# A two-layer block on one core: the scan's decays, factors of k and first inverse computed elsewhere

## The reference, cut to what matters

```python
def rwkv7_scan(r, w, k, v, kk, a):        # 16 heads of 64, 512 steps
    def step(state, inp):
        r_t, w_t, k_t, v_t, kk_t, a_t = inp
        sa = jnp.einsum('bhvk,bhk->bhv', state, -kk_t)
        state = (state * w_t[:, :, None, :] + sa[..., None] * (kk_t * a_t)[:, :, None, :]
                 + v_t[..., None] * k_t[:, :, None, :])
        return state, jnp.einsum('bhvk,bhk->bhv', state, r_t)
```

## Time and profile before

| what | us |
| --- | --- |
| runs, median of 3 | 2411.03 |
| lowest and highest run | 2410.76, 2415.05 |
| the profiled execution, its time | 2415.91 |
| its span in the profile | 2414.1 |
| PE busy | 2265.8 |
| DVE busy | 1255.7 |
| ACT busy | 934.1 |
| POOL busy | 830.2 |

### The profile page before, as it was taken

How to read it: one execution, slowest core, us unless ns; L and a number is a source line. 1 busy time by engine, 2 the same in 40 slices (tenths; PEclk the granted TensorE clock), 3 DMA queues, 4 the chain that set the end, 5 groups by cost and what they waited for, 6 DMA issues and landing times.

```text
span 2414.1 us, 46358 instructions
## 1 busy us (share of the span) xinstructions
PE 2265.8 (94%) x19576; PEld 1705.2 (71%) x19576; DVE 1255.7 (52%) x2027; ACT 934.1 (39%) x1665; POOL 830.2 (34%) x456
## 2 busy tenths in 40 slices
PE   8999999999978998888888899999998999999998
PEld 6886778888866647777777747877887766763476
DVE  5028254022164576777777515695313899736123
ACT  4238434233244433444444423464323222344133
POOL 2310334344313115444444203344441433430246
PEclk9999999999979998999999999999997999999999
DMA  4312222232302210000000122244221333222232
GB/s 143 118 51 78 70 70 88 94 99 86 105 25 78 96 42 3 10 10 10 10 10 10 38 70 70 96 183 133 94 87 63 129 113 114 87 87 79 70 90 84
DMA packets 49883, 180.71 MB, mean 75 GB/s; under 512 B 5600, under 2 KB 5856, under 8 KB 49440
## 3 DMA queue, kind: packets, MB, share of 16 engines
q1 hardware_dynamic: 46064, 166.89, 21.4%
q10 hardware_dynamic: 3632, 11.08, 1.2%
HBM read 167.39 MB, written 10.55 MB: 74 GB/s over the span
## 4 chain that ended last, share of the span: by engine, by line
PE 72%; issue 12%; DVE 7%; ACT 4%; POOL 3%; DMA 1%; POOLq 0%; ACTq 0%; SPq 0%; DVEq 0%
PE ps L596 15%; PE ps L597 15%; PE ps L598 15%; PE ps L599 6%; POOL ring_lo L2224 3%; PE ps L858 2%; PE ps L897 2%; PE ps L644 2%; PE ps L1093 1%; PE ps L888 1%; PE ps L925 1%; PE ps L715 1%; PE ps L730 1%; PE ps L705 1%; PE ps L1036 1%
## 5 line engine op out<-in xcount | busy, mean ns | idle before, releaser
L2224 POOL TENSOR_TENSOR ring_lo<-ring,ring_hi 128x1024 fp32r<-128x1024 f32 x232 | 566.0, 2448 | 1018.3 <-ACT ring_hi L1150 1018.2
L598 PE MATMUL ps<-u_lo,ring_hi 128*128 128x512 f32 x968 | 384.7, 397 | 0.0
L1150 ACT ACTIVATE ring_hi<-ring 128x1024 fp32r<-128x1024 f32 x232 | 243.3, 1053 | 113.2 <-DMA ring<-in_wall 109.9
L599 PE MATMUL ps<-arena,ring 128*128 128x512 f32 x608 | 266.1, 594 | 6.4 <-ACT arena L1595 3.3
L599 PEld LDWEIGHTS ps<-arena,ring 128*128 128x128 f32 x608 | 114.4, 190 | 154.3 <-issue 138.6
L596 PE MATMUL ps<-mlp_u_hi,ring_hi 128*128 128x512 f32 x512 | 204.9, 400 | 12.3 <-DVE u_lo L1712 8.2
L598 PEld LDWEIGHTS ps<-u_lo,ring_hi 128*128 128x128 f32 x968 | 183.8, 190 | 43.5
L596 PE MATMUL ps<-mid_hi,ring_hi 128*128 128x512 f32 x512 | 203.3, 397 | 2.6 <-POOL ring_lo L2224 2.6
L597 PE MATMUL ps<-mlp_u_hi,ring_lo 128*128 128x512 f32 x512 | 203.6, 398 | 0.0
L598 PE MATMUL ps<-mid_lo,ring_hi 128*128 128x512 f32 x512 | 202.5, 396 | 0.0
L597 PE MATMUL ps<-mid_hi,ring_lo 128*128 128x512 f32 x512 | 202.5, 395 | 0.0
(11 more groups left out here) (425 smaller groups left out, 4331.0 us busy)
## 6 DMA issues: line engine op xcount, KB each, us to landing
ring<-in_wall SPq DMA_DIRECT2D x273, 512.0 KB, 3.6
s_tables<-arena ACTq DMA_DIRECT2D x16, 512.0 KB, 2.8
arena<-s_tables SPq DMA_DIRECT2D x16, 512.0 KB, 3.6
arena<-bias_lines SPq DMA_DIRECT2D x16, 448.0 KB, 4.3
arena<-in_lora SPq DMA_DIRECT2D x8, 384.0 KB, 3.1
h<-in_x SPq DMA_DIRECT2D x1, 2048.0 KB, 8.1
out<-arena ACTq DMA_DIRECT2D x8, 256.0 KB, 2.9
consts<-in_consts SPq DMA_DIRECT2D x1, 1216.0 KB, 14.4
```

The costliest lines, as they stand in the source:

```text
L598: return nc.tensor.matmul(y, w_hi, low, start=False, stop=x == k - 1)
L599: return nc.tensor.matmul(y, ring[:, at:at + P], rhs(x), start=x == 0, stop=x == k - 1)
L1150: nc.scalar.activation(ring_hi[:, slot], ring[:, slot], ACT.Copy).then_inc(sem("weights_high"), 1)
L2224: G.tensor_tensor(ring_lo[:, slot], ring[:, slot], ring_hi[:, slot].bitcast(F32), ALU.subtract).then_inc(sem("weights_split"), 1)
```

## The change

The exponential of the decay up to the position before is no longer computed: within a chunk it is the neighbour's `ro`, and 1 at the chunk's first position. DVE reads `ro` shifted by one position when it makes `al`, and writes the chunk's first position (the last for the flipped direction) by itself. So the subtraction L1973 and the exponential L1421 go. The two exponentials left per direction are moved on ACT from levels 3 and 4 to behind the u copies of steps 0 to 3. The factor in `kd` is made by ACT (Identity with scale and bias) in level 5 behind the copy of v, in place of DVE in level 4; ACT waits there for `with_bonus` of the previous pair, since that pair's bonus lies in the same buffer. DVE's remaining feature steps move from after steps 3 to 5 to after steps 4 to 6. The predicated copy reads L from PSUM, still behind ACT's copy, and direction 0 is transposed before direction 1 is placed.

```diff
-            def decays(n, F, d):
-                act.wait_ge(sem("decay_summed"), n(2, d + 1))
-                nc.scalar.activation(F[d]["ka"], F[d]["ro"], ACT.Exp, scale=DECAY).then_inc(sem("decays_ready"), 1)
-                nc.scalar.activation(F[d]["al"], F[d]["al"], ACT.Exp, scale=-DECAY).then_inc(sem("decays_ready"), 1)
-                act.wait_ge(sem("decays_ready"), n(6, 3 * d + 1))
-                nc.scalar.activation(F[d]["ro"], F[d]["ro"], ACT.Exp, scale=-DECAY).then_inc(sem("decays_ready"), 1)
+            def decay(n, F, d, step):
+                if step == 0:
+                    act.wait_ge(sem("decay_scanned"), n(2, d + 1))
+                    nc.scalar.activation(F[d]["ka"], F[d]["ro"], ACT.Exp, scale=DECAY).then_inc(sem("decays_ready"), 1)
+                else:
+                    act.wait_ge(sem("decays_ready"), n(4, 2 * d + 1))
+                    nc.scalar.activation(F[d]["ro"], F[d]["ro"], ACT.Exp, scale=-DECAY).then_inc(sem("decays_ready"), 1)
+
+            def kd_factors(n, F):
+                for d in range(2):
+                    act.wait_ge(sem("z_taken"), n(6, 3 + d))
+                    nc.scalar.activation(F[d]["kd"], F[d]["be"], ACT.Identity, scale=pair_col("k_a", n),
+                                         bias=der[:, bass.ds(n(1, OMKA), 1)]).then_inc(sem("kd_factor"), 1)
...
             take_value(6)
-            for d in range(2):
-                decays(first, feats[0], d)
+            for k in range(4):
+                decay(first, feats[0], k // 2, k % 2)
+            kd_factors(first, feats[0])
             features(first, feats[0], 2)
...
                         ins.then_inc(sem("v_turned"), 1)
-                    if nxt and l in (3, 4):
-                        decays(nxt, G, l - 3)
+                        if prev:
+                            act.wait_ge(sem("with_bonus"), prev(2, 2))
+                        if nxt:
+                            kd_factors(nxt, G)
...
                                              ).then_inc(sem("u_taken_too"), 1)
+                    if nxt and j < 4:
+                        decay(nxt, G, j // 2, j % 2)
...
                     elif step == 1:
-                        dve.wait_ge(sem("decay_scanned"), n(2, d + 1))
-                        TT(r["al"], r["ro"], r["al"], ALU.subtract).then_inc(sem("decay_summed"), 1)
+                        dve.wait_ge(sem("decays_ready"), n(4, 2 * (d + 1)))
+                        V_.tensor_copy(ends_at[d], ends(r["ro"], d)).then_inc(sem("p_end_ready"), 1)
                     elif step == 2:
-                        dve.wait_ge(sem("z_taken"), n(6, 3 + d))
-                        TS(r["kd"], r["be"], pair_col("k_a", n), der[:, bass.ds(n(1, OMKA), 1)], ALU.mult, ALU.add
-                           ).then_inc(sem("kd_factor"), 1)
-                    elif step == 3:
-                        dve.wait_ge(sem("decays_ready"), n(6, 3 * (d + 1)))
-                        V_.tensor_copy(ends_at[d], ends(r["ro"], d)).then_inc(sem("p_end_ready"), 1)
-                    elif step == 4:
-                        STT(out=r["al"], in0=r["al"], scalar=-1.0, in1=pair_tile(kk, n), op0=ALU.mult, op1=ALU.mult
-                            ).then_inc(sem("al_ready"), 1)
+                        to, at, first = [(slice(1, CH), slice(0, CH - 1), 0), (slice(0, CH - 1), slice(1, CH), CH - 1)][d]
+                        al, by = chunks(r["al"]), chunks(pair_tile(kk, n))
+                        STT(out=al[:, :, to], in0=chunks(r["ro"])[:, :, at], scalar=-1.0, in1=by[:, :, to],
+                            op0=ALU.mult, op1=ALU.mult)
+                        TS(al[:, :, first], by[:, :, first], -1.0, None, ALU.mult).then_inc(sem("al_ready"), 1)
                     else:
                         dve.wait_ge(sem("p_end_ready"), n(2, d + 1))
+                        dve.wait_ge(sem("al_ready"), n(2, d + 1))
...
                     V_.copy_predicated(chunks(R[d]["TT"]), mask("level", d * LEVELS).bitcast(mybir.dt.int32),
-                                       chunks(R[d]["L"])).then_inc(sem("tt_started"), 1)
-                for d in range(2):
+                                       chunks(bank(4 * d + 1))).then_inc(sem("tt_started"), 1)
                     dve.wait_ge(sem("tt_started"), n(2, d + 1))
                     V_.transpose(R[d]["T"], R[d]["TT"]).then_inc(sem("t_started"), 1)
...
-                    if nxt and l in (1, 2):
-                        features(nxt, G, p_end[1 - parity], l - 1)
+                    if nxt and l == 1:
+                        features(nxt, G, p_end[1 - parity], 0)
...
-                        if nxt:
-                            features(nxt, G, p_end[1 - parity], 2)
...
-                    if nxt and 3 <= j < 6:
-                        features(nxt, G, p_end[1 - parity], j)
+                    if nxt and 4 <= j < 7:
+                        features(nxt, G, p_end[1 - parity], j - 3)
...
-                        pool.wait_ge(sem("decays_ready"), n(6, 3 * (d + 1)))
+                        pool.wait_ge(sem("decays_ready"), n(4, 2 * (d + 1)))
```

More of the change, by code:

```diff
@@ L2086, in pair @@
                         out_bonus(n, F, j // 2)
-                    if nxt and 3 <= j < 6:
-                        features(nxt, G, p_end[1 - parity], j)
+                    if nxt and 4 <= j < 7:
+                        features(nxt, G, p_end[1 - parity], j - 3)
             first, last = (lambda per, c=0: c), (lambda per, c=0: (DT - 1) * per + c)
-            for step in range(6):
+            for step in range(4):
                 features(first, feats[0], p_end[0], step)
```

## The result

The changed kernel takes 2418.97 us, the median of 12 runs, beside 2410.9 for the kernel before in the same session. The ratio is 1.0026, with a 95% interval of 1.0015 to 1.0037: by this ratio it is slower by 6.3 us (0.0026 of 2410.9), over the 0.2% that can be told, where 3.9 us less were forecast. The forecast range ended at 2416.5. The profiled execution took 2419.43 us, near its median.

The account below looks back on a forecast made before the run. PE, busy 94% of the span, was taken as the bound. Terms -10.5 -0.7 -4.0 +5.5 +2.5 +3.3 sum to -3.9 us, giving 2407.1 us against the median 2411.03; range 2400.0 to 2416.5.

Parts of the forecast that it names:

- Part 1: Start of each inverse: copy from PSUM and earlier transpose let PE start sooner; -1.5 us a pair, -10.5 in seven.
- rival E: Start of each inverse: predicated copy as slow from PSUM, gain there only -4.2; total 2413.4 us, chance 0.12.
- Parts 2 and 3: Inverse levels: subtraction between levels 2 and 3 gone, -0.7 us; exponentials out of levels 3 and 4, -4.0 us.
- part 3: Level 5: PE's wait for ACT's copy behind three exponentials goes; -4.0 us, bounds -5.1 and -2.0.
- Part 4: Ahead of step 0's w copy: factors of k on ACT delay PE; +0.8 us a pair, +5.5 in seven.
- Part 5: State steps: POOL's later features slow step 3's decays, +0.4; together +0.35 us a pair, +2.5 in seven.
- Part 6: First pair, outside the loop: later factor delays POOL's features and first L858; +3.3 us, bounds +2.3 and +5.0.
- Rival C: State steps 1 and 3: POOL blocks DVE's decays, 18.9 us in place of 2.5; total 2423.5 us, chance 0.08.
- rival D: ACT's Identity needs a table load of its own in seven pairs, +10.8 us; total 2417.9 us, chance 0.03.
- B: Costs at ACT's factors, state steps and first pair mostly hidden, full level-5 gain; -10.3 us, 2400.7 us, chance 0.15.

Follow-up runs that it names:

- factor_on_dve: The kernel after with the factor of k back on DVE, all else of the change kept: 2398.1 us, ratio 0.9935 to before.
- placed_from_psum_alone: The kernel before with only the predicated copy from PSUM and direction 0 transposed ahead of direction 1's copy: ratio 0.9962 to before.
- Experiment 10: factor_on_dve with the two exponentials of each direction back in levels 3 and 4: ratio 0.9953 to before.
- experiment 9: factor_on_dve with only the first pair's factor on ACT, behind the four Exp ahead of the loop: ratio 0.9958 to before.
- factor_in_step0: The kernel after with both factors on ACT moved behind step 0's u copies, ahead of that step's Exp: ratio 0.9985 to before.
- first_factor_on_act: The kernel of experiment 9: factor_on_dve with only the first pair's factor on ACT; ratio 0.9958 to before.
- exp_in_levels: The kernel of Experiment 10: factor_on_dve with the exponentials back in levels 3 and 4; ratio 0.9953 to before.
- one_idle_identity: factor_on_dve plus one ACT Identity, its result unread, ahead of step 0's w copies: ratio 0.9926 to before.
- two_idle_identities: factor_on_dve plus two ACT Identities, their results unread, ahead of step 0's w copies: ratio 0.9986 to before.
- factor_on_act_alone: The kernel before with only the factor of k moved to ACT, in the loop and ahead of it: ratio 1.0100 to before.
- gap_filled: The kernel after plus six unread PE products behind step 0's w products, filling PE's wait: ratio 1.0006 to before.
- two_idle_gap_filled: two_idle_identities plus six unread PE products filling PE's wait ahead of step 0: ratio 0.9965 to before.

## Why the prediction was wrong

**Part 1: right, a little less than forecast.** -9.2 measured in eight pairs; 1.5 each would be -12.0, less the 1.3 that came back as a wait for ACT. The measurement's interval holds it. Copies of 0.69 to 0.74, masks of 2.50 and a wait of 1.3 in place of 12.5 were all as forecast; rival E falls. The Trainium skill ("SBUF — State Buffer", "Who interferes with whom") says that a VectorE instruction with at most one SBUF input, outside the modes in which it uses both port pairs, does not contend with GpSimd. 16 copies of 16 here agree; the prediction gave the rule without the exception.

**Parts 2 and 3: right as far as the runs tell, not taken apart.** factor_on_dve lies 0.0027 below placed_from_psum_alone, 6.5 us, from two sessions and with intervals that overlap by 0.0003; their forecast was 4.7. The wait of L897 for ACT (5.1 us) is gone, and PE's issue waits at L888, L858 and L897 grew by 1.0 in sum (19.3 to 20.3), where I had let 1.1 fall due. Experiment 10 puts part 3 at 4.3 against its 4.0, within a wide interval.

**Part 4: the failed step.** The prediction said: "with two I take 0.65, 1.3 for both factors. Less the idle 0.5: +0.8 us, in seven pairs +5.5." The mechanism was right and nearly so the size: the Identities start 0.72 apart and take 0.81, and the wait of L1014 grew by 7.6 us over the pairs, where the term had 5.5 and its bound 7.5. The Trainium skill's 0.71 apart ("ScalarE: Activation LUTs", "What ACT_TABLE_LOAD costs") was nearer than my 0.65, and its +6.4 nearer than my +5.5. What failed is that the wait was taken for the whole price. The idle time lies just ahead of PE's densest stretch, and with it the clock falls in six of seven pairs: 14.2 us of longer steps in the profiled execution. The prediction named such a stretch as something that would move the time, and gave it neither a term nor a chance. The profile of before had a warning: its one fall between the levels and the state steps came right behind the 1.33 us wait for ACT that the prediction itself reads from the earlier trace rows. Part 4 then put waits of that length ahead of step 0 in seven pairs.

**Part 5: right in sign, wrong in place.** I put +0.4 at step 3 and -0.2 at step 1. In the pair at 1277 us POOL's products do meet step 3's decays, which take 0.95 us, but that step still lasts 2.67: it stayed within its slack. The loss is in steps 1 and 2, 0.9 a pair once the clock is full, against 0.4 before: +0.5 where the sum had +0.35. In the kernel after most of it lies under the slower clock, so 14.2 and 5.5 must not be added.

**Part 6: right.** The first L858 starts at 914.3 where 915.4 was forecast (912.13 before), and experiment 9's 5.5 stands beside the forecast's 4.8.

**The sum.** By the experiments: what stays in factor_on_dve is -15.7 (my parts 1 to 3: -15.2, or -16.7 with the first pair); the delay +7.6, by PE's wait; the first pair +5.5. These make -2.6, close to the forecast of -3.9, by terms of which each is known to a few us only. From there to the measured +6.3 are 8.9 us, and the rows hold about that for the clock: 14.2 of long steps less the 1.7 that before had, less some 0.4 in each of six pairs for the POOL conflict that the slow clock covers, makes 10.1. Rival C, the slow one with most weight, is false for the kernel after as a whole; its mechanism, not its full price, shows in factor_in_step0; rival D is false (three table loads a pair, as before); B asked for costs that were all there.

## What to carry to other kernels

A short stall of TensorE can have two prices: its length, and what follows for its clock in the dense work right behind it. Before placing work on the path into such a stretch, look at the granted clock in each of its occurrences, and where it falls in one of them, at what the engine waited for just ahead. Here that was 1.33 us for ACT in one pair of before, and 1.35 us put ahead of step 0 in seven pairs cost more than their length. And where one engine is relieved (DVE here, which had slack), ask whether the engine that takes the work stands on the path at that point: here the two products were free on DVE and cost 22 us on ACT.

## What the hardware did that I had not expected

How often the clock fell at the start of the state steps, by PE's idle time just ahead of step 0's L1014:

| idle ahead of step 0 | kernel | pairs at half clock |
|---|---|---|
| 0.3 us | factor_on_dve, first_factor_on_act, exp_in_levels | 0 of 7 each |
| 0.3 us | factor_in_step0 | 1 of 7, behind a wait of 1.48 in step 1 |
| 0.3 us | before, placed_from_psum_alone | 1 of 7 each, behind a wait of 1.33 in level 5 |
| 0.6 us | one_idle_identity | 2 of 7 |
| 1.3 us | two_idle_identities | 5 of 7 |
| 1.3 us | factor_on_act_alone | 7 of 7 |
| 1.4 us | after | 6 of 7 |
| filled with six products | gap_filled, two_idle_gap_filled | 0 of 7 each |

The idle figures are PE's longest wait there over the pairs of each kernel. Six falls cost 14.2 us after the change, 2.4 each, beside 1.35 of idle time that came with one. The same code fell in some pairs and not in others, 18 of 21 at 1.3 to 1.4 us. The Trainium skill says ("TensorE: Matmul & The Clock Gate", "A second HAM failure mode: psum-queue depth-cycling") of one measured kernel that short idle stretches of the engine between groups of products came often enough for its clock to swing between the two levels. The rows here show the same two levels, but for a single stall of 1.3 us once in some 60 us, behind a stretch of small products with waits of their own.

The length of the stall alone does not decide it. In the kernel before PE stands 1.6 us ahead of the inverse's first L858 in six pairs, and so it does in factor_on_act_alone, and the 5 us behind each of these 12 stalls read a granted clock of 1.00, like the window at 1157.90 above. What makes the place ahead of step 0 different stays open: PE also waits 0.3 to 0.5 us for v's copy (L996) there, just ahead of the stall, and no run changed that.

The other surprise is that a slower clock hid another loss: with the clock restored in gap_filled, 14 us of long steps went, and the time fell by only 4.8 by the ratios: POOL's conflict took 5.5 back, and the six added products some 2.0. That leaves 6.7, which the intervals (1.0015 to 1.0037, 0.9997 to 1.0015) allow. The two profiled executions are 8.9 apart, which is what their first three steps differ by over the seven pairs (15.3 us over 2.67 each after the change, 6.4 in gap_filled).
